# A third seven-product pair in the SwiGLU feed forward, with all its weight sums made earlier and kept in DRAM

## The reference

```python
merged = jax.nn.sigmoid(ga) * (y_a @ w_up_a[layer]) + jax.nn.sigmoid(gb) * (y_b @ w_up_b[layer])
x = x + merged @ w_out[layer]
h = rmsnorm(x, norm_ffn[layer])
x = x + (jax.nn.silu(h @ w_gate[layer]) * (h @ w_up[layer])) @ w_down[layer]
```

## Time and profile before

| | |
|---|---|
| time, median of 3 runs | 721.14 us (720.99 to 721.19) |
| time of the profiled execution | 720.66 us |
| its span | 718.9 us |
| granted TensorE clock, mean | 0.999 |
| PE busy | 709.1 us, 99% |
| DVE busy | 555.8 us, 77% |
| ACT busy | 424.6 us, 59% |
| POOL busy | 25.9 us, 4% |
| transfers | 152.22 MB, mean 212 GB/s |

### The profile page before, as it was taken

How to read it: one execution, slowest core, us unless ns; L and a number is a source line. 1 busy time by engine, 2 the same in 40 slices (tenths; PEclk the granted TensorE clock), 3 DMA queues, 4 the chain that set the end, 5 groups by cost and what they waited for, 6 DMA issues and landing times.

```text
span 718.9 us, 9667 instructions
## 1 busy us (share of the span) xinstructions
PE 709.1 (99%) x3722; PEld 567.9 (79%) x3722; DVE 555.8 (77%) x949; ACT 424.6 (59%) x701; POOL 25.9 (4%) x43
## 2 busy tenths in 40 slices
PE   8999999999999999999999999999999999999996
PEld 4678885588888888888888777778888888888885
DVE  4789999898666757756998799855857988678933
ACT  4487658995754654546645677666456466436712
POOL 1030012001000000000010000000000000000000
PEclk9999999999999999999999999999999999999999
DMA  9996939617556585744548433344375598568501
GB/s 366 415 378 224 387 104 357 218 59 263 197 179 231 214 289 196 268 146 154 163 144 300 172 118 118 119 172 178 118 233 175 197 313 310 181 230 316 209 1 58
DMA packets 71932, 152.22 MB, mean 212 GB/s; under 512 B 4096, under 2 KB 19456, under 8 KB 70864
## 3 DMA queue, kind: packets, MB, share of 16 engines
q1 hardware_dynamic: 70080, 146.32, 57.4%
q0 software_dynamic: 1520, 5.03, 2.0%
...
## 4 chain that ended last, share of the span: by engine, by line
PE 91%; ACT 3%; issue 2%; DMA 2%; DVE 1%; POOL 0%; POOLq 0%; DVEq 0%; SPq 0%
PE bank L511 23%; PE bank L513 23%; PE bank L512 23%; PE bank L856 5%; PE bank L493 5%; PE bank L854 3%; DMA W<-in_w_in 2%; ACT WH L1185 1%; PE bank L530 1%; PE bank L988 1%; PE bank L1010 1%; PE bank L694 1%; PE bank L716 1%; PE bank L570 1%; PE bank L853 1%
## 5 line engine op out<-in xcount | busy, mean ns | idle before, releaser
L1720 DVE TENSOR_TENSOR WL<-W,WH 128x1024 fp32r<-128x1024 f32 (+2 forms) x234 | 263.4, 1173 | 27.0 <-ACT WH L1185 26.7
L1185 ACT ACTIVATE WH<-W 128x1024 fp32r<-128x1024 f32 (+2 forms) x234 | 222.9, 1013 | 55.7 <-DMA W<-in_w_mlp 35.8
L511 PE MATMUL bank<-WH,AHL 128*128 128x512 f32 (+1 forms) x440 | 173.1, 393 | 0.0
L513 PE MATMUL bank<-WH,AHL 128*128 128x512 f32 (+1 forms) x440 | 169.7, 386 | 0.0
L512 PE MATMUL bank<-WL,AHL 128*128 128x512 f32 (+1 forms) x440 | 169.6, 385 | 0.0
L511 PEld LDWEIGHTS bank<-WH,AHL 128*128 128x128 f32 x440 | 82.7, 188 | 19.0 <-issue 3.2
L513 PEld LDWEIGHTS bank<-WH,AHL 128*128 128x128 f32 x440 | 82.6, 188 | 16.9
L512 PEld LDWEIGHTS bank<-WL,AHL 128*128 128x128 f32 x440 | 82.8, 188 | 15.4
L511 PE MATMUL bank<-WH,HH 128*128 128x512 f32 (+1 forms) x218 | 84.9, 390 | 0.0
L513 PE MATMUL bank<-WH,HL 128*128 128x512 f32 (+1 forms) x218 | 84.5, 388 | 0.0
L512 PE MATMUL bank<-WL,HH 128*128 128x512 f32 (+1 forms) x218 | 84.4, 387 | 0.0
...
## 6 DMA issues: line engine op xcount, KB each, us to landing
W<-in_w_mlp SPq DMA_DIRECT2D x32, 1024.0 KB, 5.4
W<-in_w_in SPq DMA_DIRECT2D x24, 1024.0 KB, 5.1
W<-in_w_down SPq DMA_DIRECT2D x11, 1024.0 KB, 5.1
W<-in_w_ada SPq DMA_DIRECT2D x10, 1024.0 KB, 8.0
WX<-in_w_ada SPq DMA_DIRECT2D x10, 1024.0 KB, 10.0
W<-in_w_out SPq DMA_DIRECT2D x8, 1024.0 KB, 5.2
W<-in_w_up SPq DMA_DIRECT2D x8, 1024.0 KB, 5.1
...
```

The source lines that it names most:

```text
L511: e.matmul(po, hs, wh[:, k, c0:c0 + cw], start=first and k == 0, stop=False, skip_group_check=onto)
L513: ins = e.matmul(po, ls, wh[:, k, c0:c0 + cw], start=False, stop=last and k == unit.nk - 1, skip_group_check=onto)
L1185: e.activation(m.WH[unit.slot][:, c], m.W32[unit.slot][:, c], ACT.Copy).then_inc(S["w_hi"], 1)
L1720: e.tensor_tensor(m.WL[unit.slot][:, c], m.W32[unit.slot][:, c], m.WH[unit.slot][:, c].bitcast(F32), ALU.subtract).then_inc(S["w_lo"], 1)
```

## The change

PAIRS becomes (2, 5, 8), so that the groups are 0, 1, 2+3, 4, 5+6, 7, 8+9, 10: three pairs, and the last group but one is now a pair. None of the weight sums are made in the ring any more. They are made earlier in 12 steps (`kept_sums` on DVE), four for each pair, and kept in a new DRAM tensor `sums`. For a step POOL loads 512 KB of w_up_2 and 512 KB of w_gate_2 into a free buffer (`blocks_in`), DVE runs four subtractions of 128 x 512, and POOL stores the 1 MB result. SUMS_AT says how many steps DVE does at each of 13 places: eight steps lie in the first block's feed forward (places 0 to 8), and four in the output stage (places 9 to 12: after `merge_a(1, 1)`, after `merge_b(0, 1)`, within `norm_features(4, 0, ...)`, and behind the `lo()` that follows `norm_scale(1, 11, ...)`). The output stage's two buffers lie at offsets 68 and 76, where the forms FS are written later. `sums_stored` therefore makes DVE wait for the last stores before the first form. SP loads the stored sums as ordinary units.

As group 2 is now a pair, its forms move ahead on DVE and ACT, before the second half of group 1. In the part `begin`, a pair's next group may also be a pair, which does not occur with these PAIRS. The semaphores res1, res2 and res3 become one, `res`. After the last pair, `up2` of the last group's first half runs before the turn of `hid`, and PE then goes straight to `down2(NG - 2, 0, ...)`.

```diff
+        self.sums = {o: M(f"sums{o}", o, [128, 4, 512]) for o in (0, 8, 68, 76)}
...
@@ -208,7 +209,13 @@
 M1_AT = {ct: 2 * i + 2 for i, ct in enumerate(M1_ORDER)}
 M2_ORDER = [(c, tb) for c in range(6) for tb in range(2)] + [(6, 0), (7, 0), (6, 1), (7, 1)]
 M2_AT = {ct: 4 * i + 4 for i, ct in enumerate(M2_ORDER)}
-PAIRS = (3,7)
+PAIRS = (2, 5, 8)
+STORED = (2, 5, 8)
+STEPS = (8, 0, 4)
+SUMS_AT = (1, 0, 2, 1, 1, 1, 2, 0, 0, 1, 1, 1, 1)
+SUMS = [[(0, 8)[s % 2] for s in range(STEPS[0])], [0] * STEPS[1], [(68, 76)[s % 2] for s in range(STEPS[2])]]
+SUM_SEM = [{0: 0, 8: 1, 68: 0, 76: 1}[o] for phase in SUMS for o in phase]
+SUM_AT = [48 * sum(b == SUM_SEM[s] for b in SUM_SEM[:s]) for s in range(len(SUM_SEM))]
 GROUPS = [(c, c in PAIRS) for c in range(11) if c - 1 not in PAIRS]
 NG = len(GROUPS)
...
     def quad_unit(g, n, src, i):
         c0 = 256 * GROUPS[g][0]
         add(("gu", g), src, 4 * i, 4, [(src, c0, 512)], True, ("gu_mm", QUAD_AT[g] + n + 1))
-        return units[-1]
+        if GROUPS[g][0] in STORED and n in (1, 2, 4, 6):
+            s = STORED.index(GROUPS[g][0])
+            kept = d["sums"][s, {4: 0, 2: 1, 1: 2, 6: 3}[n]].rearrange("p (k n) -> p k n", k=4)
+            units[-1].pieces = [(0, 512, kept)]
...
-            at = len(units)
-            down_units(g - 1)
-            down = units[at:]
-            quad_unit(g, 2, "w_up_2", 1)
+            if not kept:
+                at = len(units)
+                down_units(g - 1)
+                down = units[at:]
+                quad_unit(g, 2, "w_up_2", 1)
+            else:
+                down_units(g - 1)
+                quad_unit(g, 2, "w_up_2", 1)
             quad_unit(g, 3, "w_up_2", 1)
             quad_unit(g, 4, "w_up_2", 0)
             quad_unit(g, 5, "w_gate_2", 1)
             quad_unit(g, 6, "w_gate_2", 1)
-            b11, t1, t2, b22, t3, b21, t4 = by["gu", g]
-            loads += [b11, t1, t2, *down, t4, b22, t3, b21]
+            if kept:
```

```diff
         unit = units[n]
         for old in unit.old:
             w.wait_ge(old.free[0], old.free[1])
+        for sem, value in unit.kept:
+            w.wait_ge(sem, value)
...
+
+    def blocks_in(phase, i):
+
+        s = sum(STEPS[:phase]) + i
+        place, landing = m.sums[SUMS[phase][i]], S[f"l_sums{SUM_SEM[s]}"]
+        if SUM_AT[s]:
+            w.wait_ge(landing, SUM_AT[s])
+        if i < 2 and phase == 0:
+            w.wait_ge(*((S["n_turned"], 4), (S["kn"], 4))[i])
+        elif phase == 1:
+            w.wait_ge(S["n_turned"], 8)
+        elif phase == 2:
+            w.wait_ge(S["pv2"], 8)
+        c0, kt = 256 * STORED[s // 4], s % 4
+        for j, src in enumerate(("w_up_2", "w_gate_2")):
+            rows = d[src][:, c0:c0 + 512].rearrange("(h k p) n -> p k h n", h=2, p=128)[:, kt, :, :]
+            e.dma_start(place[:, 2 * j:2 * j + 2, :], rows).then_inc(landing, 16)
+
+    def kept_sums(phase):
+
+        ahead = len(set(SUMS[phase]))
+        for i in range(ahead):
+            blocks_in(phase, i)
+        for i in range(STEPS[phase]):
+            s = sum(STEPS[:phase]) + i
+            w.wait_ge(S["made"], 4 * s + 4)
+            kept = d["sums"][s // 4, :, :, 512 * (s % 4):512 * (s % 4) + 512].rearrange("i p n -> p i n")
+            e.dma_start(kept, m.sums[SUMS[phase][i]][:, :, :]).then_inc(S[f"l_sums{SUM_SEM[s]}"], 16)
+            if phase == 2 and i in (1, 2):
+                power(9 + i)
+            if i + ahead < STEPS[phase]:
+                blocks_in(phase, i + ahead)
...
     power(5)
-    w.wait_ge(S["res1"], 8)
+    w.wait_ge(S["res"], 8)
     e.dma_start(m.g1b[:, :], d["final_g"].to_broadcast([128, D])).then_inc(S["l_gain"], 16)
+    kept_sums(0)
     power(6)
     power(7)
     power(8)
     power(9)
     w.wait_ge(S["btw"], 12)
     e.dma_start(m.g2b[:, :], d["norm_final"].to_broadcast([128, D])).then_inc(S["l_gain"], 16)
-    for i in range(10, 14):
-        power(i)
+    kept_sums(1)
+    kept_sums(2)
+    power(12)
+    power(13)
 
```

```diff
@@ -1148,7 +1210,8 @@
             hid_turn2(g, 1)
             if g < NG - 2:
                 begin(g + 1)
-    up2(NG - 1, 0)
+    if not GROUPS[NG - 2][1]:
+        up2(NG - 1, 0)
     down2(NG - 2, 0, False, False, (0,))
     hid_turn2(NG - 1, 0)
...
     silu_gate(1, 0, 0)
     hi()
+    if GROUPS[2][1]:
+        for i in range(4):
+            form_hi(i)
     silu_gate(0, 1)
```

```diff
@@ -2091,6 +2163,7 @@
         e.tensor_copy(m.AH[:, 0:4, ts], hv).then_inc(S["n_dve"], 1)
         w.wait_ge(S["n_dve"], n + 1)
         tt(m.AL[:, 0:4, ts], hv, m.AH[:, 0:4, ts].bitcast(F32), ALU.subtract, "kn")
+        between()
         w.wait_ge(S["n_act"], 5 * call + 5)
...
+    def sums_stored():
+
+        for b in range(2):
+            w.wait_ge(S[f"l_sums{b}"], max([0, *(SUM_AT[s] + 48 for s in range(made["n"]) if SUM_SEM[s] == b)]))
+
+    def kept_sums(place):
+
+        for s in range(sum(SUMS_AT[:place]), sum(SUMS_AT[:place + 1])):
+            at = m.sums[sum(SUMS, [])[s]]
+            u0, u1, g0, g1 = (at[:, i, :] for i in range(4))
+            w.wait_ge(S[f"l_sums{SUM_SEM[s]}"], SUM_AT[s] + 32)
+            tt(g0, u0, g0, ALU.subtract, "made")
+            tt(u0, u1, u0, ALU.subtract, "made")
+            w.wait_ge(S["made"], 4 * s + 1)
+            tt(u1, u1, g0, ALU.subtract, "made")
+            w.wait_ge(S["made"], 4 * s + 3)
+            tt(g1, g1, u1, ALU.subtract, "made")
+            made["n"] = s + 1
+
+    made = {"n": 0}
...
             gate_rows(2 * c - 3)
         else:
             gate_add()
+        kept_sums(c)
...
@@ -2384,11 +2484,13 @@
     merge_a(0, 1)
     merge_a(1, 0)
     merge_a(1, 1)
+    kept_sums(9)
     lo()
     merge_b(0, 0)
     lo()
     merge_b(1, 0)
     merge_b(0, 1)
+    kept_sums(10)
     merged_lo(0)
     lo()
...
-    residual(0, 0, "out2_mm", 3, "res2")
-    residual(1, 0, "out2_mm", 4, "res2")
+    residual(0, 0, "out2_mm", 3, "res")
+    residual(1, 0, "out2_mm", 4, "res")
     norm_scale(0, 10, (16, 17))
-    norm_features(4, 0, m.ffn, None)
-    residual(0, 1, "out2_mm", 7, "res2")
+    norm_features(4, 0, m.ffn, None, lambda: kept_sums(11))
+    residual(0, 1, "out2_mm", 7, "res")
     lo()
-    residual(1, 1, "out2_mm", 8, "res2")
+    residual(1, 1, "out2_mm", 8, "res")
     norm_scale(1, 11, (18, 19))
     lo()
+    kept_sums(12)
 
```

```diff
+        if not near:
+            first_hidden()
         w.wait_ge(S["silu"], SILU_AT[g, 1])
         tt(m.hid[g % 2][:, 1, :], m.u1, m.rel[1][:, :], ALU.mult, "hid2")
-        lo(2)
+        if near:
+            hid_lo2(g, 0)
+            lo()
+            hid_lo2(g, 1)
+            lo()
+        else:
+            lo(2)
+            for tb in range(2):
+                hid_lo2(g, tb)
...
     gated(1, 0, 0)
-    lo()
+    sums_stored()
+    if GROUPS[2][1]:
+        form(0)
+        form(1)
+        lo()
+        form(2)
+        form(3)
+    else:
+        lo()
     gated(0, 1)
     hid_lo2(0, 0)
     lo(2)
     gated(1, 1, 1)
     hid_lo2(0, 1)
-    lo()
-    for i in range(4):
-        form(i)
+    if GROUPS[2][1]:
+        for i in range(4):
+            form_lo(i)
+        lo()
+    else:
+        lo()
+        for i in range(4):
+            form(i)
     for tb in range(2):
         hid_lo2(1, tb)
-    for i in range(4):
...
+    if not GROUPS[2][1]:
+        for i in range(4):
+            form_lo(i)
```

More of the change, by code:

```diff
@@ L359, in weight_units @@
         unit.lo = (S["w_lo"], 2 * u)
-    for n, g in enumerate(g for g in range(NG) if GROUPS[g][1]):
+    for n, g in enumerate(g for g in range(NG) if GROUPS[g][1] and GROUPS[g][0] not in STORED):
         t1, t2, _, t3, _, t4 = by["gu", g][1:]
@@ L363, in weight_units @@
             unit.base = unit.landed
-        t1.landed, t2.landed, t4.landed, t3.landed = ((S["made"], 8 * n + 2 * i + 2) for i in range(4))
+        t1.landed, t2.landed, t4.landed, t3.landed = ((S["made"], 4 * len(SUM_SEM) + 8 * n + 2 * i + 2) for i in range(4))
     return units, loads, by
@@ L1091, in down2 @@
             for i, unit in enumerate(by["dn", g]):
-                part(unit, m.HH[g % 2], m.HL[g % 2], 2 * i, tb, 2 * n + tb, first and i == 0, last, "dn_mm",
+                part(unit, m.HH[g % 2], m.HL[g % 2], 2 * i, tb, 2 * n + tb, first and i == 0, last and i == GROUPS[g][1], "dn_mm",
                      lambda k: ("hid_lo", 16 + 2 * g + tb + 1), 512 * n, 512)
@@ L1677, in scalar_program @@
             hi()
-        for tb in range(2):
-            hid_hi2(g, tb)
+            for tb in range(2):
+                hid_hi2(g, tb)
     hi()
@@ L2502, in vector_program @@
     hid_lo2(0, 1)
-    lo()
-    for i in range(4):
-        form(i)
+    if GROUPS[2][1]:
+        for i in range(4):
+            form_lo(i)
+        lo()
+    else:
+        lo()
+        for i in range(4):
+            form(i)
     for tb in range(2):
         hid_lo2(1, tb)
-    for i in range(4):
-        form_lo(i)
+    if not GROUPS[2][1]:
+        for i in range(4):
+            form_lo(i)
     for g in range(2, NG - 1):
```

(4 more changed lines are left out.)

94 lines of the change are left out of this document (62 added, 32 removed).

## The result

The changed kernel takes 735.85 us (median of 4 runs, 733.53 to 737.81) against 721.07 us (720.99 to 721.19) before: a ratio of 1.0204, 95% interval 1.0173 to 1.0235. The direction was forecast. The size was not: +14.8 us against a forecast of +8.0, and outside the range, which ended at 732.5.

A forecast was written before the change was run, and what follows sets the result against it. The prediction took PE's own stream of matmuls as the bound. New PE waits of 10.75 us less 2.72 saved gave +8.0 us on a median of 721.14, so 729.1 us, with a range of 723.5 to 732.5.

The forecast's parts named there:

- What PE saves: On PE, a third pair replaces 96 matmuls by 84; 12 fewer save 2.72 us, the whole possible gain.
- The price of a step: On DVE, a step's four operations of 128 x 512 take 2.56 us, and twelve steps take 31 us.
- Eight steps in the first feed forward: DVE's idle time and 12 us of slack on the weight splits cover these steps: no PE wait.
- The burst of transfers: First feed forward: some 4 MB after two steps in a row, beside weight loads, about 12 us; taken as 0.
- Step 8: Ahead of `merge_b`: DVE finishes the half that `merged_turn(0)` needs late, and PE waits 2.1 us.
- step 9: Between `mrg` and its split: the split comes late for `out2(0, 0)`, and PE waits 1.4 us.
- Step 11: Ahead of the second norm's features: the first AL half comes late for `up2(0, 1)`, and PE waits 1.4 us.
- The forms' wait for the store: Forms wait 5.2 us for POOL's 1 MB store, so PE waits 1.75 us at `down2(0, 1)`; least certain term.
- The end: Last pair's `hid` split loses its cover of 24 matmuls: PE waits 3.6 us, then 0.5 for the last group's `hid`.
- rival B: Only the end and part of the rest show, output stage waits may halve: 725.2 us, chance 0.2.
- rival C: Slow POOL transfers: 8.3 us for the 1 MB store, forms start 3.1 us later: 732.2 us, chance 0.13.
- rival D: First feed forward's transfer burst holds weight loads beyond 12 us: PE waits up to 3 us more, 732.1 us, chance 0.08.

The follow-up runs named there:

- best: Changed kernel with the third pair's sums in the ring, the end's matmul cover put back and the gate rows' addition ahead of two weight splits: 718.67 us.
- gate_first: Changed kernel with DVE's addition of the gate rows moved ahead of the two weight splits that stood before it: 733.33 us.
- step5: Changed kernel with the sixth step moved one chunk ahead in the first feed forward: 735.94 us.
- noend_fill: noend with 12 extra matmuls, whose result nobody reads, on PE in the wait at the end: 722.45 us.
- noend: best without the end's matmul cover, so with the wait at the end alone: 724.85 us.
- allkept: Changed kernel, all twelve steps kept, with the end's cover, the gate rows' addition moved ahead and the last step beside the one before it: 724.33 us.

## Why the prediction was wrong

- **What PE saves, 2.72 us: right.** best shows 2.50.
- **The price of a step, 2.56 us: right.** The four operations take 304.24 - 301.71 = 2.53 us to the next row.
- **Eight steps in the first feed forward, nothing: wrong, 1.9 us.** This step failed. I took the weights split from 234.71 as the thing that PE needs first, and gave all eight steps their 12 us of slack. The weights had it. `gate_add` did not: before, its first half was done at 316.72 + 0.69 = 317.41, only 1.4 us ahead of the matmul at 318.85 that takes its bank, and from step 5 on DVE has only its waits of about 1 us for ACT's turn-round between it and `gate_add`, which no lead can shorten. gate_first showed it by moving that one instruction pair. The burst of transfers, which I had named as the weak point, cost PE nothing where the steps stood. Where step5 put two steps in a row, the input came late and g2b's wait was 1.8 us longer.
- **Step 8, 2.1, and step 9, 1.4: right** (1.9 and 1.2).
- **Step 10, nothing: right.**
- **Step 11, 1.4: mis-sized, 2.1.** DVE's delay was as priced; the norm's chain was late by 0.7 more, because ACT waited for a weight load beside the step's own input. I had not costed that queue.
- **The forms' wait for the store, 1.75: right as a mechanism, hidden in this kernel's trace.** DVE's wait is there, and the landing time was near (4.8 against 5.2). The 0.7 of the line above moved DVE, its store and PE alike. The 1.7 of the clock below moved PE alone, and used the wait up. In gate_first and step5, where the clock stayed up, the wait stands at 1.75 and 2.2. That it is 1.75 to the hundredth is luck, since the store took 5.1 us there and PE's wait at the second norm was 2.3.
- **The end, 3.6 and 0.5: right** (3.4 and 0.2; with the restart of PE 3.8 in the pair best and noend_fill).
- **"The clock stays at its upper level": wrong.** I wrote a falling clock under what would make the prediction wrong, and gave it no term and no chance. This is the second step that failed. For the end alone noend and noend_fill give 2.4 us. In the profiled run the one fall costs 1.6 to 1.7 us where it stands. But it took the place of the store's wait: the stretch around both is 24.7 us with the fall and 25.1 in gate_first without it, so that here the missing term added nothing to the forecast's 1.75. Between runs the four at 733.53, 734.29, 737.41 and 737.81 had mean clocks of 0.995, 0.993, 0.993 and 0.989: the order fits, but two runs of one clock lie 3.1 us apart, and in allkept the fastest run has the lowest clock. The mean also counts the end of the span, where no matmul runs any more (in allkept the last one starts at 715.06, and the clock is at its lower level from 717.3). So how much of the spread is the clock is not shown; that it goes where PE has no wait (best, 0.6 us) and with the filled wait (noend_fill, 1.2 in 11 runs) is.

The sum for the profiled run by the table: 0.4 at the start, 2.2 at g2b (wait and restart), 0.5 up to the output stage, 3.7 for steps 8 and 9, 4.0 for step 11 with its clock, 0.2, then 3.8 and 0.3 at the end less 2.7: 12.4 of the 12.8 us between the spans. Against the forecast of 8.0 that is 2.2 for g2b, 0.9 for the start and the stretch up to the output stage, and 1.1 for the second norm with what follows (4.2 against 1.4 + 1.75); the rest is rounding and small differences. The median is another 2.3 above that run, and which waits and falls the slower runs had was not traced. The 0.4 and 0.5 have no cause shown: small waits for transfers and for DVE and ACT rows of the first 60 us come and go between kernels that are alike there.

Where rival B put the time (some waits halved) nothing points; rival C's transfers were not slow at the store (4.8 us), although the median from issue to landing of all twelve stores is 8.9, most of them beside weight loads; rival D was wrong in its mechanism and near in its size.
